# Seven-product pairs in all groups of a macaron FFN, on unscaled activations

## The reference

```
def rmsnorm(x, w):
    y = xf * lax.rsqrt(jnp.mean(xf * xf, axis=-1, keepdims=True) + EPS)
    return (y * w).astype(x.dtype)
def swiglu(x, w_gate, w_up, w_down):
    return (jax.nn.silu(x @ w_gate) * (x @ w_up)) @ w_down
x = x + 0.5 * swiglu(rmsnorm(x, norm_w[l, 0]), ffn_w_gate[l, 0], ffn_w_up[l, 0], ffn_w_down[l, 0])
```

## Time and profile before

| what | us |
|---|---|
| median of 3 runs (2213.06 to 2216.58) | 2214.12 |
| the profiled execution, its own time | 2216.74 |
| its span, from first to last instruction | 2215.0 |
| PE busy (98% of the span) | 2176.4 |
| DVE busy (65%) | 1433.1 |
| ACT busy (40%) | 885.8 |
| DMA, mean | 91 GB/s |

### The profile page before, as it was taken

One profiled execution on the slowest core, in us unless ns is written; L12 is line 12 of the kernel. 1 busy time (PEld: TensorE's weight loads), 2 busy tenths in 40 slices (PEclk: granted clock), 3 DMA queues, 4 the chain that ended last, 5 costly groups with the idle time before them and its releaser, 6 DMA issues.

```text
span 2215.0 us, 40643 instructions
## 1 busy us (share of the span) xinstructions
PE 2176.4 (98%) x16504; PEld 2154.1 (97%) x16504; DVE 1433.1 (65%) x2131; ACT 885.8 (40%) x1366; POOL 45.7 (2%) x50
## 2 busy tenths in 40 slices
PE   7999999999999999999999999999999999999997
PEld 7999999999999999999999999999999899999997
DVE  5488657685555468848655884864766454788485
ACT  4235435354533334525423452544322432345252
POOL 0000000001100000000000000000011100000000
PEclk9999999999999999999999999999999999999999
DMA  5222322223332222222322222232122222223222
GB/s 185 77 81 89 114 67 86 96 88 130 108 114 77 95 77 81 90 87 88 109 80 76 86 95 95 81 100 88 47 96 87 95 77 95 76 86 104 76 86 72
DMA packets 72566, 201.42 MB, mean 91 GB/s; under 512 B 7268, under 2 KB 26980, under 8 KB 72448
## 3 DMA queue, kind: packets, MB, share of 16 engines
q1 hardware_dynamic: 72448, 199.80, 27.6%
HBM read 187.82 MB, written 11.95 MB: 90 GB/s over the span
## 4 chain that ended last, share of the span: by engine, by line
PE 93%; DVE 4%; ACT 2%; issue 1%; DMA 0%; POOL 0%; DVEq 0%; SPq 0%; ACTq 0%; POOLq 0%
PE ps L476 55%; PE ps L533 27%; PE ps L750 4%; PE ps L605 1%; DVE w_lo L1715 1%; PE ps L781 1%; PE ps L770 1%; PE ps L784 0%; PE ps L800 0%; ACT w_hi L1182 0%; PE ps L614 0%; PE ps L793 0%; PE ps L628 0%; PE ps L794 0%; DVE x L2514 0%
## 5 line engine op out<-in xcount | busy, mean ns | idle before, releaser
L476 PE MATMUL ps<-h_lo,w_hi 128*128 128x288 f32 x1616 | 350.9, 294 | 4.1 <-DVE h_hi L2179 4.1
L476 PE MATMUL ps<-h_hi,w_hi 128*128 128x288 f32 x1616 | 350.7, 294 | 2.5 <-DVE w_lo L1715 1.6
L476 PE MATMUL ps<-xn_hi,w_hi 128*128 128x288 f32 x1536 | 337.3, 298 | 12.4 <-DVE w_lo L1715 11.5
L476 PE MATMUL ps<-xn_hi,w_lo 128*128 128x288 f32 x1536 | 332.1, 294 | 0.0
L476 PE MATMUL ps<-xn_lo,w_hi 128*128 128x288 f32 x1536 | 331.8, 294 | 0.0
L1715 DVE TENSOR_TENSOR w_lo<-raw,w_hi 128x1024 fp32r<-128x1024 f32 x220 | 259.4, 1221 | 56.7 <-ACT w_hi L1182 54.5
L476 PE MATMUL ps<-h_hi,w_lo 128*128 128x288 f32 x1360 | 294.0, 293 | 0.0
L476 PEld LDWEIGHTS ps<-xn_hi,w_hi 128*128 128x128 f32 x1536 | 248.1, 189 | 20.5 <-issue 18.0
L476 PEld LDWEIGHTS ps<-h_lo,w_hi 128*128 128x128 f32 x1616 | 261.6, 189 | 4.8 <-DVE h_hi L2179 4.5
L476 PEld LDWEIGHTS ps<-h_hi,w_hi 128*128 128x128 f32 x1616 | 261.5, 189 | 3.5 <-DVE w_lo L1715 1.8
L533 PE MATMUL ps<-th_lo,w_hi 128*128 128x288 f32 x896 | 264.2, 295 | 0.0
(11 more groups left out here) (276 smaller groups left out, 3731.1 us busy)
## 6 DMA issues: line engine op xcount, KB each, us to landing
raw<-in_w_gate SPq DMA_DIRECT2D x88, 512.0 KB, 3.2
raw<-in_w_up SPq DMA_DIRECT2D x88, 512.0 KB, 4.3
raw<-in_w_down SPq DMA_DIRECT2D x64, 512.0 KB, 3.6
raw<-in_w_mix SPq DMA_DIRECT2D x64, 512.0 KB, 4.3
raw<-in_w_down SPq DMA_DIRECT2D x32, 384.0 KB, 3.2
state_s<-in_state_c SPq DMA_DIRECT2D x4, 1024.0 KB, 7.1
out_c_s<-state_s SPq DMA_DIRECT2D x4, 1024.0 KB, 4.5
state_s<-in_state_g SPq DMA_DIRECT2D x4, 1024.0 KB, 6.3
```

Of the source, the lines that this page charges most:

```text
L476: ins = nc.tensor.matmul(o, a, b[:, c] if c is not None else b, start=first and j == 0, stop=last and j == 2)
```

## The change

- In group 0 of each FFN pairs 5 to 8 become seven-product pairs; pairs 1 to 4 stay plain.
- The activations stay unscaled: `t_sums` goes. In its place come `u_even` (ACT: even feature tile of x times the norm weight), `u_sums` and `u_low` (DVE) and `u_high` (ACT), in four steps among pairs 1 to 4 of group 0: one after the weights of pair 2, two after those of pair 4, one before the weight sums of pair 5. xn_hi and xn_lo are not touched.
- rstd comes in at the end of each seven-product pair (`rows_scale`, two DVE multiplications).
- The additions of partial results change: ACT copies a bank into another bank of PSUM, and PE adds its next product on top (`start=False`); one 576-column DVE addition is left instead of four of 288. Since two of these banks are accumulated into before PE ever opened them in an FFN, `open_banks` issues two matmuls ahead of pair 5.
- The high and low parts of the first weights are made by one 1024-column instruction for two units instead of two of 512.
- At the program's start ACT does a small copy that brings its table load ahead of x, and the squares follow the first weights. The last down phase loses its `by_bank` order.

```
             def g_phase(j, ph):
...
+                else:
+                    for i, half, sums in ((0, 0, (0,)), (0, 1, ()), (1, 0, (1, 2)), (1, 1, (3,))):
+                        if (i, half) != (1, 1):
+                            split_next(j, i, half)
+                        for pp in sums:
+                            u_sums(ph, pp)
+                            u_low(ph, pp)
+                        if (i, half) == (1, 1):
+                            sums_early(ph, 2, 0)
+                        dve.wait_ge(pe_done, ph["base"] + 2 * i + half + 1)
+                        if i == half == 0:
+                            norm_rstd(ph["norm"])
+                        evac_g(ph, i, half)
...
             def d_phase(j, ph):
                 for pp in range(4):
...
-                    if ph["group"] == 0:
-                        for n in ((0, 1), (2,), (3,), ())[pp]:
-                            t_sums(ph, n)
...
-                own(V.tensor_tensor(T2(3), xn_hi[:, xs, :].bitcast(f32), xn_lo[:, xs, :].bitcast(f32), ALU.add))
-                V.tensor_tensor(T2(3), T2(3), bcast_mid(rstd[:, :], 2), ALU.mult).then_inc(t_ready, 1)
...
+            def u_sums(ph, pp):
+
+                n = 4 * ph["ffn"] + pp
+                even, odd, w_odd = T(3 + pp % 2), x[:, 2 * pp + 1, :], norm_w[:, ph["norm"], 2 * pp + 1:2 * pp + 2]
+                dve.wait_ge(even_ready, n + 1)
                 if pp:
+                    dve.wait_ge(u_lo_done, n)
+                own(V.tensor_tensor(T(0)[:, FIRST], even[:, SECOND], even[:, FIRST], ALU.subtract))
+                V.scalar_tensor_tensor(T(1)[:, FIRST], odd[:, SECOND], w_odd, even[:, SECOND], ALU.mult, ALU.subtract)
+                own(V.scalar_tensor_tensor(T(0)[:, SECOND], odd[:, SECOND], w_odd, T(0)[:, FIRST], ALU.mult,
+                                           ALU.subtract))
+                V.scalar_tensor_tensor(T(1)[:, SECOND], odd[:, FIRST], w_odd, T(0)[:, SECOND], ALU.mult,
+                                       ALU.subtract).then_inc(u_sum, 1)
+
+            def u_low(ph, pp):
+
+                n = 4 * ph["ffn"] + pp
+                dve.wait_ge(u_sum, n + 1)
+                dve.wait_ge(u_hi_done, n + 1)
...
+                V.tensor_tensor(th_lo[:, :, pp, :], T2(0).rearrange("p a (c n) -> p (a c) n", c=2),
+                                th_hi[:, :, pp, :].bitcast(f32), ALU.subtract).then_inc(u_lo_done, 1)
+                dve.wait_ge(u_lo_done, n + 1)
...
+            def rows_scale(ph, i, half):
+
+                m = 2 * i + half
+                dve.wait_ge(pe_done, ph["base"] + m + 1)
+                V.tensor_tensor(cut2(T(0)), ps[:, 4 * half:4 * half + 2, FIRST], cut2(rstd[:, :]), ALU.mult)\
+                    .then_inc(gate_ready, 1)
+                dve.wait_ge(part_ready, ph["seven"] + m + 1)
+                V.tensor_tensor(T(1), T(1), rstd[:, :], ALU.mult).then_inc(up_ready, 1)
...
             def seven_rest(j, ph, i, half, last):
...
                 act.wait_ge(product_done, 6 * w + 2)
+                product_copy(P7_COPY, half, 3)
                 act.wait_ge(raw_full[2 * half + 1], 8 * (pair - half) + 16)
                 unit_high(half, 1, raw_tiles(half, 1, 1)).then_inc(hi_done, 1)
                 act.wait_ge(product_done, 6 * w + 3)
-                product_copy(U2_COPY, half)
+                product_copy(ps[:, 4 * half + 2, FIRST], half, 1)
                 unit_high(half, 2, by_tile(S4)).then_inc(unit_hi, 1)
...
                 if consumer:
                     iteration(0, first_norm=True, bank_wait=ph["base"] > 0, by_bank=(1,))
-                    with pe.Fori(1, ph["pairs"] // 2) as i:
-                        iteration(i)
...
+                    iteration(2, seven=True, opened=False)
+                    iteration(3, seven=True)
```

More of the change, by code:

```diff
@@ L48, in schedule @@
                 out.append(dict(kind="G", pairs=k, base=pair, ffn=ffn, norm=norm, k=KT_X, k0=k0,
-                                group=g, hidden=hidden, seven=seven, plain=hidden - seven))
-                pair, hidden, seven = pair + k, hidden + k, seven + (k if g else 0)
+                                group=g, hidden=hidden, seven=seven - (0 if g else 4), plain=4 * ffn,
+                                scaled=seven - (0 if g else 4)))
+                pair, hidden, seven = pair + k, hidden + k, seven + (k if g else k - 4)
                 out.append(dict(kind="D", pairs=4, base=pair, ffn=ffn, norm=norm, k=k, k0=k0,
@@ L577, in phase, with open_banks, iteration @@
                 consumer = ph["kind"] == "G" and ph["group"] == 0
-                seven = ph["kind"] == "G" and ph["group"] > 0
-                def iteration(i, first_norm=False, bank_wait=True, by_bank=()):
+                def open_banks():
+                    for bank in (0, 2):
+                        nc.tensor.matmul(ps[:, bank, FIRST], xn_hi[:, 0, 0:P], xn_hi[:, 0, FIRST], start=True,
+                                         stop=True)
+                def iteration(i, first_norm=False, bank_wait=True, seven=False, opened=True, by_bank=()):
                     for half in range(2):
@@ L585, in iteration @@
                             pe.wait_ge(psum_free, pair - 1)
+                        if not opened and half == 0:
+                            open_banks()
                         ins = seven_pair(ph, i, half) if seven else feature_pair(ph, i, half, half in by_bank)
@@ L1245, in seven_rows @@
                 m = 2 * i + half
[L1246 to L1250 removed]
+                w, pair = ph["seven"] + m, ph["base"] + m
+                act.wait_ge(gate_ready, w + 1)
+                nc.scalar.activation(T(0), T(0), ACT.Silu).then_inc(gate_done, 1)
                 if not last:
@@ L1288, in evac_g, with u_even, u_high @@
                     .then_inc(hh_done, 1)
+            def u_even(ph, pp):
+                act.wait_ge(ssq_done, 4 * ph["norm"] + 3)
+                if pp >= 2:
+                    act.wait_ge(u_sum, 4 * ph["ffn"] + pp - 1)
+                nc.scalar.activation(T(3 + pp % 2), x[:, 2 * pp, :], ACT.Copy,
+                                     scale=norm_w[:, ph["norm"], 2 * pp:2 * pp + 1]).then_inc(even_ready, 1)
+            def u_high(ph, pp):
+                act.wait_ge(u_sum, 4 * ph["ffn"] + pp + 1)
+                nc.scalar.activation(th_hi[:, :, pp, :], T2(0).rearrange("p a (c n) -> p (a c) n", c=2), ACT.Copy)\
+                    .then_inc(u_hi_done, 1)
             def g_phase(j, ph):
                 n = ph["pairs"] // 2
-                def iteration(i):
-                    for half in range(2):
-                        split_next(j, i, half)
-                        if ph["group"] == 0 and half == 0 and i is 0:
-                            norm_root(ph["norm"])
-                        evac_g(ph, i, half)
                 def seven_iteration(i, last=False):
@@ L1645, in last_down @@
                 half_root(1)
+            act.wait_ge(zero_done, 1)
+            nc.scalar.activation(rstd[SAMPLE:P, 0:1], vs_lo[SAMPLE:P, 0:1].bitcast(f32), ACT.Copy)
             act.wait_ge(norm_in, 16)
@@ L1707, in own, with split @@
                 dve.wait_ge(dve_chain, chain[0])
-            def split(ph, i, half):
+            def split(ph, i, half, blocks=range(2)):
                 pair = ph["base"] + 2 * i + half
-                for blk in range(2):
+                for blk in blocks:
                     slot = 2 * half + blk
@@ L1807, in seven_pair @@
-                dve.wait_ge(copy_done, 3 * w + 1)
-                dve.wait_ge(product_done, 6 * w + 2)
-                part(T(0)[:, FIRST], half, 0, P1_COPY)
-                dve.wait_ge(unit_hi, 5 * w + 5)
+                if not last:
+                    dve.wait_ge(unit_lo, 3 * w + 2)
+                    sum_1(after[1])
+                dve.wait_ge(unit_hi, 3 * w + 3)
                 unit_low(half, 2, by_tile(S4)).then_inc(unit_lo, 1)
                 if last:
-                    split(PHASES[j + 1], 0, 0)
+                    split(PHASES[j + 1], 0, 0, (0,))
@@ L1814, in seven_pair @@
                 else:
-                    dve.wait_ge(unit_lo, 5 * w + 4)
-                    sum_1(ph, *after)
                     sum_2(ph, *after)
-                dve.wait_ge(copy_done, 3 * w + 2)
-                dve.wait_ge(product_done, 6 * w + 4)
-                part(T(4)[:, SECOND], half, 2, U2_COPY)
-                if not last:
-                    dve.wait_ge(unit_lo, 5 * w + 5)
+                    dve.wait_ge(unit_lo, 3 * w + 3)
                     sum_4(ph, *after)
-                dve.wait_ge(copy_done, 3 * w + 3)
@@ L1902, in g_phase @@
                 n = ph["pairs"] // 2
-                def iteration(i):
-                    for half in range(2):
-                        split_next(j, i, half)
-                        dve.wait_ge(pe_done, ph["base"] + 2 * i + half + 1)
-                        if ph["group"] == 0 and half == 0 and i is 0:
-                            norm_rstd(ph["norm"])
```

(1 more changed line is left out.)

220 lines of the change are left out of this document (105 added, 115 removed).

## The result

The changed kernel takes **2228.14 us** (median of 4 runs, 2226.44 to 2229.48); the kernel before, run beside it, 2213.59 (4 runs, 2212.62 to 2216.58). The ratio is 1.0061, with a 95% interval of 1.0049 to 1.0073: slower by 0.6%, clear of the 0.2% that a measurement can tell, and 2.1 us above the top of the range. The profiled execution is one of 2228.10 us; against that of before (2216.74, 3.2 above its median) it is 11.4 longer, which leaves 14.5 between the medians.

The account below looks back on a forecast made before the run. The prediction took TensorE's matmuls as the bound, with DVE a hair behind in seven-product pairs. It summed -22.1 + 14.2 + 6.8 + 3.8 = +2.7 us, so a median of 2216.8 us, range 2205 to 2226.

Parts of the forecast that it names:

- Part 1: Group 0, pairs 5 to 8: fewer matmuls as plain pairs turn seven-product, -22.1 us; bank opening free, or 1.0 without a wait.
- Part 2: Group 0, before pair 5: preparation steps on DVE make PE wait 3.7 us once and 3.5 three times, +14.2 us.
- Rival (a): Preparation steps cost DVE 3.4 us instead of 4.7, ACT's copy hidden; no wait before pair 5, 2196 us; chance 0.1.
- Part 3: Behind the four waits before pair 5: PE's clock falls to half for 3.4 us, 1.7 us each, +6.8 us.
- Rival (b): The clock holds behind the four new waits, so the 6.8 us fall away: 2210 us; chance 0.2.
- Part 4: End of group 2, before the last down phase: h_lo comes 0.95 us later in each FFN, +3.8 us.
- Part 5: Seven-product pairs: the ring through DVE and ACT takes 11.27 us against PE's 11.10; cost 0, bounds 0 and +11.
- rival (c): Seven-product pairs: a ring of 11.45 us instead of 11.27 delays PE, +11 us, 2228 us; chance 0.2.

Follow-up runs that it names:

- run 6: The changed kernel with the preparation steps interleaved (step 3 in buffers of its own), the same operations: 2211.92 us.
- run 4: The kernel before, TensorE's group 0 written out, with a long wait before pair 5 until pair 4's h_lo is written: 2249.06 us.
- run 5: The kernel before, TensorE's group 0 written out, with a short wait before pair 5 until DVE has read pair 4's banks: 2230.73 us.
- run 8: The changed kernel with group 0 all plain pairs again, the preparation steps spread over its pairs 3 to 6: 2221.91 us.
- run 10: The interleaved changed kernel with the second half-block of the first pair bank by bank in the down phases of groups 0 and 1: 2203.42 us.
- run 11: The kernel before, with the second half-block of pair 2 of group 0 no longer run bank by bank: 2227.34 us.

## Why the prediction was wrong

**Part 1, fewer matmuls: right.** Without the waits (run 6) pairs 5 to 8 take 179.1 us against 199.7: -20.6, that is -22.1, the 1.0 for opening the banks that the text named for this case, and 0.5 since a seven-product pair takes 11.126 us where before it took 11.099.

**Part 2, the preparation steps: right.** 12.8 us of waits (3.54, 3.08, 3.09, 3.09) where 3.7 and 3 x 3.5 were forecast. The way to it was right too: run 6 hides ACT's round trips in the same steps and the waits vanish. Rival (a) had named exactly this as what would decide.

**Part 3, the clock: partly right, and its net by luck within the bounds.** Three of the four waits were followed by 3.4 us at half the clock. The one at 758.41 was not, with the same 3.1 us idle as two that were. The stretches behind the waits of FFNs 2 and 3, the granted clock third from the right:

```profile
758.40:761.80 3.40, 3.39 (x26) 3.40 (x27) 3.09 (x4) 1.66 (x4) 0.00 (x0) 1.00 0.48 154
1156.10:1159.50 3.40, 3.40 (x16) 3.40 (x16) 2.85 (x4) 1.25 (x3) 0.00 (x0) 0.50 0.46 159
```

A fall cost 1.5 us and not 1.7 (16.24 against 14.69 for pair 5; 13.78 in the changed kernel against 12.24 in run 6 for the first pair of the last down phase): 4.6 us of the 6.8. The wait of 2.48 us at the end had one too, +1.5; two falls in the mixers went, -3.0, though the waits ahead of them, 2.06 and 2.2 us, are as long in both kernels. The net is 3.2 us. Rival (b) was wrong in substance, and its time, 2210, is far off.

**Part 4, the end of group 2: right.** 1.11 instead of 0.30 us, three times, and 2.48 instead of 1.59: 3.3 us of the 3.8.

**Part 5, the ring: right at 0.** No seven-product pair was held up; rival (c) came near the measured time, 2228, by a mechanism that did not occur.

**What failed is a term that the sum did not have.** The step is the sentence of the first part, "so both run at 0.13 us a matmul" (the rows give 130.0 ns for the plain pair and 132.1 for the seven-product pair). It took the pace as a constant, so that phases whose matmuls the change leaves alone cost nothing. They cost 10.2 us (32 down pairs x 0.32), 0.6 in pairs 3 and 4 of FFN 1 behind the wait there, and 1.4 in groups 1 and 2. With the measured terms the sum closes: -22.1 + 1.0 + 0.5 (part 1), + 12.8, + 3.2, + 3.3, and these 12.2, is +10.9. Another 1.2 lies in the longer distances behind the waits (0.2 at each of the four before pair 5, 0.1 at three last down phases), the earlier start of FFN 1 (-2.2) and its wait before pair 3 (+2.1) nearly cancel, and 0.3 is gained at the very end: +11.7 against the 11.6 between the last matmul starts. What set the pace in these phases is shown in part: that a wait ahead of plain pairs brings the slow one (runs 4 and 5), and that the new seven-product pairs leave it behind even where no wait stood (runs 6 and 8); which of their differences does it stays open.

The trace of before had the second pace in it: 12.48 us for the pairs of one down phase, and 9.60 for 72 matmuls, 133.3 ns each, in the last one. I had not divided one by the other.

## What to carry to other kernels

Divide the time of a stretch without waits by its matmuls, phase by phase, before pricing anything on a TensorE-bound kernel: a spread of 2 to 3% between phases of equal matmuls can be a state of the engine that an edit elsewhere gives or takes, here with one small edit in either direction (the phases concerned: 7.9 us less in run 10 than in run 6, 12.9 more in run 11 than before). A wait costs more than its length when such a state hangs on it (run 5: 1.7 us cost 4.3). And where an added preparation step makes TensorE late, look at what its queue waits for between its halves first: interleaving the same instructions was worth 16 us (run 6).
